# Loading x in both layouts and joining two projection tiles in the token quarters of a one-core transformer block

## The reference, cut to what matters

```
h = rms_norm(x, norm_mix_g)                  # x: 1024 tokens x 1024 features
proj = h @ w_in                              # 3584 columns and 8 gate columns
a_q, a_k, a_v, d_qkv, d_z, d_beta, d_alpha = split(proj)
a_out = rms_norm(chunked_band_attention(a_q, a_k, a_v))
d_qkv = silu(causal_depthwise_conv(d_qkv))   # 4 taps
q, k = l2norm(d_q) * Dk ** -0.5, l2norm(d_k) # per head of 128
o = gated_delta_rule(q, k, d_v, d_beta, d_alpha)
x = x + concat(a_out, gated rms_norm(o)) @ w_out
h = rms_norm(x, norm_ffn_g)
x = x + (silu(h @ w_gate) * (h @ w_up)) @ w_down
```

## Time and profile before

| | us |
|---|---|
| median of the runs | 1279.91 |
| the profiled execution | 1279.22 |
| its span | 1277.3 |
| PE busy | 1259.2 |
| POOL busy | 769.7 |
| DVE busy | 750.7 |
| ACT busy | 585.5 |

### The profile page before, as it was taken

One profiled execution on the slowest core, in us unless ns is written; L12 is line 12 of the kernel. 1 busy time (PEld: TensorE's weight loads), 2 busy tenths in 40 slices (PEclk: granted clock), 3 DMA queues, 4 the chain that ended last, 5 costly groups with the idle time before them and its releaser, 6 DMA issues.

```text
span 1277.3 us, 18239 instructions
## 1 busy us (share of the span) xinstructions
PE 1259.2 (99%) x6892; PEld 1056.4 (83%) x6892; DVE 750.7 (59%) x1031; ACT 585.5 (46%) x941; POOL 769.7 (60%) x523
## 2 busy tenths in 40 slices
PE   8999999999999999999999999999999999999998
PEld 7888888888887889888887888888888888888887
DVE  5565656846927767743687665565654566445452
ACT  6587645653137765652452333333333324544441
POOL 4354567764526563552258996889877875655541
DMA  5721355531135015532213355443244427985663
GB/s 185 252 63 35 92 148 143 138 108 50 35 64 176 3 45 185 182 136 109 73 51 115 155 208 190 178 161 142 117 161 190 189 110 268 315 296 182 202 194 147
DMA packets 83806, 184.86 MB, mean 145 GB/s; under 512 B 20920, under 2 KB 33280, under 8 KB 76680
## 3 DMA queue, kind: packets, MB, share of 16 engines
q1 hardware_dynamic: 78000, 179.96, 41.6%
q10 hardware_dynamic: 5720, 3.74, 1.0%
HBM read 129.31 MB, written 56.98 MB: 146 GB/s over the span
## 4 chain that ended last, share of the span: by engine, by line
PE 87%; DVE 5%; ACT 3%; issue 2%; POOL 2%; DMA 1%; ACTq 0%; DVEq 0%
PE ps L2301 29%; PE ps L392 23%; PE ps L2326 16%; PE ps L415 6%; PE ps L2104 2%; PE ps L2138 1%; PE ps L2126 1%; PE ps L2067 1%; PE ps L2084 1%; DVE SX L1864 1%; PE ps L377 1%; POOL WR L868 1%; PE ps L2207 1%; PE ps L2092 1%; ACT L1146 1%
## 5 line engine op out<-in xcount | busy, mean ns | idle before, releaser
L392 PE MATMUL ps<-HT,SPLIT 128*128 128x512 f32 (+1 forms) x1392 | 317.6, 385 | 0.0
L392 PEld LDWEIGHTS ps<-HT,SPLIT 128*128 128x128 f32 x1392 | 252.7, 188 | 49.3
L2326 PE MATMUL ps<-S,HI 128*128 128x512 f32 x616 | 189.8, 389 | 0.0
L1053 POOL TENSOR_TENSOR S<-RAB,S 128x512 fp32r<-128x512 f32 x77 | 107.6, 1401 | 90.7 <-ACT S L1226 90.4
L2326 PEld LDWEIGHTS ps<-S,HI 128*128 128x128 f32 x616 | 115.6, 188 | 24.1
L2301 PE MATMUL ps<-S,WR 128*128 128x512 f32 x516 | 120.5, 390 | 0.4 <-POOL WR L868 0.4
L2326 PE MATMUL ps<-S,LO 128*128 128x512 f32 x308 | 120.0, 389 | 0.0
L1742 DVE TENSOR_TENSOR LO<-RAB,HI 128x512 fp32r<-128x512 f32 x77 | 66.8, 878 | 90.3 <-ACT HI L1223 90.3
L2301 PE MATMUL ps<-HI,WR 128*128 128x512 f32 x360 | 115.1, 390 | 0.2 <-POOL WR L868 0.2
L2301 PEld LDWEIGHTS ps<-S,WR 128*128 128x128 f32 x516 | 96.8, 188 | 20.8 <-POOL WR L868 0.8
L2301 PE MATMUL ps<-HI,WX 128*128 128x512 f32 x344 | 112.8, 390 | 0.7 <-ACT UV L1191 0.7
(11 more groups left out here) (289 smaller groups left out, 2553.8 us busy)
## 6 DMA issues: line engine op xcount, KB each, us to landing
hidden<-HB SPq DMA_DIRECT2D x11, 1792.0 KB, 6.6
RAB<-hidden SPq DMA_DIRECT2D x77, 256.0 KB, 3.1
RAW<-units SPq DMA_DIRECT2D x36, 512.0 KB, 4.0
RAWG<-w_gate SPq DMA_DIRECT2D x11, 1024.0 KB, 10.8
RAWU<-w_up SPq DMA_DIRECT2D x11, 1024.0 KB, 4.9
RAWD<-w_down SPq DMA_DIRECT2D x11, 1024.0 KB, 8.8
down_t<-RAWD SPq DMA_DIRECT2D x11, 1024.0 KB, 3.9
RAB<-down_t SPq DMA_DIRECT2D x44, 256.0 KB, 3.5
```

What stands on the lines that cost most here:

```text
L392: mm = pe.matmul(ps[:, bank + a // HALF, a % HALF:a % HALF + width], w, right[other][:, k, a:a + width], start=(k == order[0] and part == ...
L1053: pool.tensor_tensor(down_b(q, 1), RAB[:, q % RAWS, 1, :], down_b(q, 0).bitcast(F32), ALU.subtract).then_inc(R["b_lo"], 1)
L2326: mm = pe.matmul(ps[:, bank + t, :], down_a(q, part)[:, t * P:(t + 1) * P], down_b(q, other), start=(p == 0 and i in (1, 6, 5, 7) and part ...
```

## The change

x comes from memory a second time as `x_t`, in which each token tile lies with its features on the partitions (the host rearranges the array). PE no longer turns x. Instead DVE writes the reciprocals of the roots on the diagonal of a 128x128 matrix (L361 of the new kernel), PE multiplies it with ones (L367), which spreads each token's value over all partitions, DVE multiplies the loaded x_t by that (L374), ACT rounds the product into the high part (L381) and DVE subtracts for the low part (L386). SP loads two tiles of x, then the same two of x_t, and so on; the first unit of the projection follows the first four transfers, and the second unit the next four.

Tile 1 of the projection is multiplied in token quarters too, in the order of `FIRST_UNITS`. The gate columns go to PSUM bank 2. The wait of the second unit's split for the scaled token tiles is gone. In `project` the side sums of tiles 0 to 6 move to between the blocks of the tile two further on (`SIDE_SUM_AT`), and the small gate products from tile 1 to tile 2. ACT copies tiles 0 and 1 out of PSUM before it applies Silu to tile 0; DVE runs the taps of tiles 0 and 1 before the split of tile 0.

```diff
+        XT = PROJ[:, 1:1 + NT, :].rearrange("p m (k c) -> p m k c", c=P)
+        RDIAG = PROJ[:, 17:19, 0:P]
...
+        def inp_diag(dve, m):
+            dve.wait_ge(nrm["inp"]["root"], m + 1)
+            dve.reciprocal(rstd[:, m:m + 1], ssq[:, m:m + 1]).then_inc(nrm["inp"]["rstd"], 1)
+            dve.wait_ge(nrm["inp"]["rstd"], m + 1)
+            ge(dve, nrm["inp"]["spread"], m - 1)
+            dve.tensor_scalar(RDIAG[:, m % 2, :], ident[:, :], rstd[:, m:m + 1], None, ALU.mult).then_inc(nrm["inp"]["diag"], 1)
+        def inp_spread(pe, m):
+            pe.wait_ge(nrm["inp"]["diag"], m + 1)
+            ge(pe, nrm["inp"]["scaled"], m - 1)
+            pe.matmul(ps[:, m % 2, 0:P], ones[:, :], RDIAG[:, m % 2, :],
+                      start=True, stop=True).then_inc(nrm["inp"]["spread"], 1)
+        def inp_scale(dve, m):
+            dve.wait_ge(xt_in[m], 16)
+            dve.wait_ge(nrm["inp"]["spread"], m + 1)
+            dve.tensor_tensor(XT[:, m, :, :], XT[:, m, :, :],
+                              ps[:, m % 2, 0:P].unsqueeze(1).to_broadcast([P, KT, P]),
+                              ALU.mult).then_inc(nrm["inp"]["scaled"], 1)
+        def inp_hi(act, m):
+            act.wait_ge(nrm["inp"]["scaled"], m + 1)
+            act.activation(HT[:, 0, :, tokens(m)], XT[:, m, :, :], ACT.Copy).then_inc(nrm["inp"]["hi"], 1)
+        def inp_lo(dve, m):
+            dve.wait_ge(nrm["inp"]["hi"], m + 1)
+            dve.tensor_tensor(HT[:, 1, :, tokens(m)], XT[:, m, :, :], HT[:, 0, :, tokens(m)].bitcast(F32),
+                              ALU.subtract).then_inc(nrm["inp"]["lo"], 1)
...
-        INP_NORM_DVE = [("scale", 0), ("scale", 1), ("lo", 0), ("lo", 1), ("scale", 2), ("scale", 3), ("lo", 2), ("lo", 3),
+        INP_NORM_DVE = [("diag", 0), ("diag", 1), ("scale", 0), ("scale", 1), ("lo", 0), ("lo", 1),
+                        ("diag", 2), ("diag", 3), ("scale", 2), ("scale", 3), ("lo", 2), ("lo", 3),
...
+        FIRST_UNITS = [("gates", 0), ("spread", 1), ("tile_0", 0), ("gates", 1), ("tile_0", 1), ("spread", 2), ("tile_1", 0),
+                       ("tile_1", 1), ("spread", 3), ("gates", 2), ("tile_0", 2), ("tile_1", 2), ("tile_0", 3), ("gates", 3),
+                       ("tile_1", 3)]
+        GATE_BANK = 2
+        SIDE_SUM_AT = {2: (7, 0), 3: (6, 1), 4: (5, 2), 5: (4, 3), 6: (3, 4), 7: (2, 5), 8: (1, 6)}
...
-                pool.wait_ge(nrm["inp"]["xn"], 2)
+                pool.wait_ge(nrm["inp"]["diag"], 2)
                 unit_split(pool, 1, 1, 0, 2)
...
                 for j in range(2, U_OUT):
-                    if j == 2:
-                        pool.wait_ge(nrm["inp"]["xn"], NT)
                     unit_split(pool, j % 2, j // 2 + 1, j - 1 if j > 2 else 0, j + 1)
...
-                columns_unit(pe, slot_of(t), 4 + 2 * slot_of(t), HTP, 0, T,
-                             {2: lambda: pre_gram_pe(pe, m), 7: lambda: pre_turn_pe(pe, m)} if 0 <= m < NT else
...
+                if t in SIDE_SUM_AT:
+                    k, n = SIDE_SUM_AT[t]
+                    between[k] = lambda: side_sum(pe, n, n, ones_r)
...
-                for t in range(1, SDV + 1):
+                for t in range(2, SDV + 1):
                     project(pe, t)
-                    side_sum(pe, t - 1, t - 1, ones_r)
+                    if t == SDV:
+                        side_sum(pe, SDV - 1, SDV - 1, ones_r)
```

More of the change, by code:

```diff
@@ L453, in hymba_block @@
         R = {n: sem("down_" + n) for n in ("hi", "a_lo", "b_lo", "block", "done", "copied", "x", "x_in")}
-        ab_in = [sem(f"down_raw_in{i}") for i in range(RAWS)]
+        ab_in = [sem(f"xt_then_down_raw_in{i}") for i in range(RAWS)]
+        xt_in = bias_in + ab_in
         NV = NPAIR * NT
@@ L695, in _ @@
             def _(sp):
-                for m in range(NT):
-                    sp.dma_start(XIN[:, m, :], x[m * P:(m + 1) * P, :]).then_inc(x_in[m], 16)
-                    if m == 1:
+                for pair in range(NT // 2):
+                    for m in (2 * pair, 2 * pair + 1):
+                        sp.dma_start(XIN[:, m, :], x[m * P:(m + 1) * P, :]).then_inc(x_in[m], 16)
+                    for m in (2 * pair, 2 * pair + 1):
+                        sp.dma_start(XT[:, m, :, :], x_t[m].rearrange("p (k c) -> p k c", c=P)).then_inc(xt_in[m], 16)
+                    if pair == 0:
                         unit_dma(sp, 1, 1)
+                    if pair == 1:
+                        sp.wait_ge(split_done, 1)
+                        unit_dma(sp, 2, 0)
                 for half in range(2):
@@ L707, in _ @@
                 sp.dma_start(dtb_row[:, :], dt_bias.partition_broadcast(P)).then_inc(small_in, 16)
-                for j in range(2, U_OUT):
+                for j in range(3, U_OUT):
                     sp.wait_ge(split_done, j - 1)
@@ L1073, in plain_tile, with conv_copy, conv_tile, conv_silu @@
                 act.activation(proj_banks(t), bank_pair(slot_of(t), 4), ACT.Copy).then_inc(banks_free, 1)
-            def conv_tile(act, t, dst, before=None):
-                act.wait_ge(unit_used, U_TILE + t + 1)
+            def conv_copy(act, t, used):
+                act.wait_ge(unit_used, used)
                 act.activation(proj_banks(t), bank_pair(slot_of(t), 4), ACT.Copy,
                                scale=taps[:, t, CONV - 1:CONV]).then_inc(conv_first, 1)
-                if before is not None:
-                    before()
+            def conv_tile(act, t, dst, before):
+                conv_copy(act, t, U_TILE + t + 1)
+                before()
+                conv_silu(act, t, dst)
+            def conv_silu(act, t, dst):
                 act.wait_ge(banks_free, U_TILE + t + 1 + BANKS0)
@@ L2032, in project @@
                 m = t - FIRST_PRE
-                columns_unit(pe, slot_of(t), 4 + 2 * slot_of(t), HTP, 0, T,
-                             {2: lambda: pre_gram_pe(pe, m), 7: lambda: pre_turn_pe(pe, m)} if 0 <= m < NT else
-                             {1: lambda: gate_turn_pe(pe, 0), 2: lambda: gate_turn_pe(pe, 2), 3: lambda: gate_turn_pe(pe, 4),
-                              4: lambda: gate_turn_pe(pe, 6)} if t == 1 else {}).then_inc(unit_used, 1)
+                between = {}
+                if t == 2:
+                    between = {k: lambda first=2 * (k - 1): gate_turn_pe(pe, first) for k in range(1, 5)}
+                if t in SIDE_SUM_AT:
+                    k, n = SIDE_SUM_AT[t]
+                    between[k] = lambda: side_sum(pe, n, n, ones_r)
+                if 0 <= m < NT:
+                    between = {2: lambda: pre_gram_pe(pe, m), 7: lambda: pre_turn_pe(pe, m)}
+                columns_unit(pe, slot_of(t), 4 + 2 * slot_of(t), HTP, 0, T, between).then_inc(unit_used, 1)
             def gate_turn_pe(pe, first):
@@ L2511 @@
         "x": np.ascontiguousarray(x[0]),
+        "x_t": _feature_tiles(np.asarray(x[0])),
         "gate_cols": _gate_columns(np.asarray(w_in[0])),
```

94 lines of the change are left out of this document (52 added, 42 removed).

## The result

| | median us | lowest to highest | profiled execution | its span | mean granted clock |
|---|---|---|---|---|---|
| before | 1279.74 (n=4) | 1278.64 to 1280.67 | 1279.22 | 1277.3 | 1.000 |
| after | 1302.08 (n=4) | 1300.84 to 1302.36 | 1301.91 | 1299.9 | 0.991 |

After takes 1.0177 times as long as before, with an interval of 1.0161 to 1.0192. The forecast was 1291.7 us, in a range of 1282 to 1295. The direction was right and the size well outside the range: +12.5 us forecast, +22.7 measured in the profiled executions.

The account below looks back on a forecast made before the run. PE was taken to bound the kernel, busy 1259.2 of 1277.3 us. Terms -0.2 + 0.65 + 0.8 + 2.0 + 7.2 + 2.3, less the old 0.3, gave +12.5 on 1279.2: 1291.7 us, range 1282 to 1295.

Parts of the forecast that it names:

- the point: End of tile 8's side sum, 136.8 us before the change; the change was priced as the shift of this point.
- the ladder: Stretch from tile 2 on, with side sums and turns of `gcum` between product blocks; forecast waits 0.65, 0.8, 2.0, 7.2, 2.3.
- tile 2, its split: Before tile 2, PE waits 0.65 us for POOL's split, whose weights are rounded only after the last gates.
- side sums of tiles 1, 2, 3, 5: Side sums wait as DVE's side chain meets POOL's work: tile 2 0.8 us, tile 3 2.0, tile 5 2.3, others nothing.
- turns of `gcum`: Behind `project(5)`, PE waits 7.2 us for the copy to `gcum`, 3.75 unhindered; the largest term.
- Rival 1: POOL doesn't hold up the side chain: 1283.1 us with the quarters hindered, 1280.3 with nothing hindered; chance 0.2.
- rival 2: A pause around the quarters brings 1.2 GHz, slowing products behind it: +3 at the middle, 1294.7 us; chance 0.12.
- The warm-up products of 186 and 119 ns: Sign for the clock: first 24 warm-up products take 186 ns each, next 16 119, so PE starts slow after idling.
- the quarters at -0.2: Tiles 0 and 1 in token quarters end at 49.9 against 50.07 us: 5 us work saved, 5 us new waits.
- Rivals 3 and 4: 3: quarters run at PE's own pace, -1.8, 1277.4 us, chance 0.05; 4: x_t comes late, 1293.3 us, chance 0.05.

Follow-up runs that it names:

- the kernel with spare turns: The changed kernel with unread transposes of `ident` filling PE's pauses (warm-up, second gates quarter, sums of tiles 3 and 5, turns of `gcum`): 1298.10 us.
- the first part alone: Against the kernel before: x in both layouts, spread by products with ones, tile 1 not joined, side sums unmoved, POOL's third-unit split held back: 1285.64 us.
- the kernel with moved turns: The changed kernel with the wait for `gcum` and its two turns moved into tile 6's projection, ahead of block 4: 1293.04 us.
- the kernel without the multiplication: The changed kernel with POOL's multiplication by the gain cut to one column per block for units 4 to 12, so results are not the reference's: 1298.94 us.
- the kernel with four edits: The changed kernel with third unit's split held, `gcum` turns in tile 6, 54 warm-up turns, spare turns ahead of sums of tiles 3 (12) and 5 (24): 1292.23 us.

## Why the prediction was wrong in size

At the point 22.24 us were lost and 12.5 forecast. Half of the 9.7 between them is the clock, which the sum left out. The clock alone doesn't bring the time into the range: with no fall it is 1296.8 us, still above 1295.

**Right: what PE waits for in the ladder.** Each wait was laid out from the earlier trace rows:

| place | forecast us | after us |
|---|---|---|
| tile 2, its split | 0.65 | 1.03 |
| side sums of tiles 1, 2, 3, 5 | 0, 0.8, 2.0, 2.3 | 0.19, 0.93, 2.07, 2.36 |
| turns of `gcum` | 7.2 | 5.15, and 7.2 with the slow stretch ahead of them gone |
| all | 12.95 | 13.7 at full clock |

The mechanism is DVE beside POOL, as the prediction had it. At full clock, in the kernel with spare turns, DVE's subtraction ends 13.7 us behind the start of the sum of tile 3, held up by POOL's multiplication, where 13.4 was laid out. Rival 1 falls: leaving out that multiplication gave 4.9 us back. The rule of the Trainium skill that the prediction drew on ("SBUF — State Buffer", Who interferes with whom) says that a VectorE instruction with two SBUF inputs contends with a GpSimd instruction that reads SBUF. The trace agrees: the low part with two SBUF sources takes 4.74 us for two beside POOL and 2.36 for two alone, where the one with a PSUM source kept to 1.22. The run with the first part alone shows that these waits come with the second part of the change. My reading is that tiles 0 and 1 end together, their side chains start one behind the other, and from there PE needs 7 blocks and a sum for each, which the chain, held up by POOL, doesn't keep up with. The 7 blocks come from `SIDE_SUM_AT` and not from the joined tile itself; no run joins the tiles and leaves the sums 8 blocks apart, so that part is argued and not shown.

**Wrong: rival 2, the clock.** This is the step that failed. I gave a fall a chance of 0.12 and 3 us, and only for the pauses in the quarters. The clock fell in both of those and twice in the ladder, and that costs 5.1 us at the point, where the sum has nothing: 3.7 in the quarters, of which 0.2 are waited out later, 1.6 behind the turns of `gcum`, and nothing behind the sum of tile 3. For the two falls in the quarters the prediction had laid out 1.2 and 4.7; they cost 2.15 and 1.56. The signs were in the prediction: two pauses of 3 and 4 us, and the waits of 7.2 and 2.3 that it had laid out itself. The warm-up products of 186 and 119 ns are a weaker one: from 2.9 to 5.0 us ten of them take 2.10 us, and the granted clock reads 1.00 there too, so what slowed them is not shown. A kernel whose longest pause in this part was 0.9 us (the prediction's 0.63 is the one before the first gates) didn't show a fall, but its clock of 1.00 spoke neither for one nor against. The Trainium skill warns of idle gaps between bursts of products ("TensorE: Matmul & The Clock Gate", Why this matters for your kernels), and the text beside rival 2 said that this made the rival likelier. The trace agrees: the clock fell behind both pauses in the quarters.

**Wrong: the quarters at -0.2.** Without the clock they end at 52.68 - 1.03 = 51.65 against 50.07 before, so +1.6. The first unit's split started at 9.94, when its transfer was there, and not at 9.1; that is 0.8, and it took the first two low parts along, each held until an instruction of POOL was through: they ended at 14.88 and not 14.0. The later low parts kept to the layout: the second gates came at 24.14 with a start 1.1 late, laid out for 22.9. The other half microsecond came behind them and is not traced.

**Left out, and put at nothing without a reason: what a pause costs beside its idle time.** A side sum that doesn't wait starts 0.15 us before the modelled end of the products ahead (147.65 against 138.10 + 9.71), and lets the next ones start 0.93 behind it; one that waits lets them start 1.04 behind. That is 0.26 for a pause, and 1.6 in all if each of the six in the ladder costs as much, which is an estimate.

The account at the point: forecast 12.5, clock 5.1, quarters 1.8, longer waits 0.8, pauses 1.6, together 21.8 of 22.24. The last 0.4 is not traced, and the 0.4 between the point and the span isn't either. Rivals 3 and 4 fall: the quarters wait for DVE, and `x_t` is waited for nowhere (the waits of PE and the releasers of DVE's scalings name PE).

## What to carry to other kernels

A wait that a change lays on TensorE can have two prices, its length and the products behind it at 1.2 GHz; these runs had the second behind pauses from 1.97 us on, though not behind each. Count it whenever the layout itself forecasts such pauses, also where the kernel before never showed a fall. Here the slow stretch ahead of a wait for a chain that was started earlier was free, and the one ahead of the work that starts the next chain was not (1.6 us). And a row of an operation with PSUM as a source says nothing of the same operation with two SBUF sources beside GpSimd; the order in which GpSimd's long instructions meet VectorE's is worth laying out, and often worth changing.

## What the runs showed of the hardware that was not expected

The length of a pause alone did not decide whether the clock fell. The pause of 2.07 us before the sum of tile 3 in after brought a fall, the one of 2.08 at the same place in the kernel with moved turns did not; 2.36 before the sum of tile 5 did not in after and did in the kernel without the multiplication; 3.02 before the sum of tile 4 did with moved turns and 3.01 did not in the kernel with four edits. The shortest with a fall behind it was 1.97 us; in this part of the kernels 1.78 and less never had one, and 3.38 and more always did. The granted clock of two kernels behind the pause before the sum of tile 4, first with moved turns (the sum starts at 118.30), then with four edits (at 113.46):

```profile
118.00:121.00 3.00, 2.70 (x9) 2.21 (x10) 2.93 (x5) 1.45 (x2) 0.00 (x0) 0.80 0.02 7
121.00:124.00 3.00, 3.00 (x11) 2.19 (x10) 2.12 (x2) 2.97 (x3) 0.00 (x0) 0.63 0.00 0
```

```profile
110.00:113.50 3.50, 0.49 (x3) 0.07 (x2) 3.47 (x4) 0.20 (x1) 2.32 (x2) 1.00 0.54 150
113.50:117.00 3.50, 3.50 (x17) 2.83 (x18) 3.43 (x4) 2.30 (x2) 0.00 (x0) 1.00 0.00 0
```

So with pauses between 2 and 3 us a kernel's time has a part that comes and goes, and one profiled execution of each kernel can't tell whether the edit did it. Executions of one kernel differ too: of thirteen of the kernel before, eight had a mean clock of 1.000 and took 1277.01 to 1278.58 us, and five had 0.998 and took 1278.97 to 1280.80. Spare turns took the fall out in every place where they filled the pause.
